# Column sums of modulation chunks: from TensorE products per accumulator to VectorE folds and shared products

## The chip, the cores and the metric

The kernel runs on one core of a Trainium2 chip. The metric is the device time of one execution in microseconds (us). Engines are named as in the profile: PE is TensorE, PEld its weight loads, DVE is VectorE, ACT is ScalarE, POOL is GpSimd, SP is the engine that issues most DMAs.

## The reference, cut to what matters

A decoder trunk of two layers on a sequence of 512 tokens with 1024 channels. Each layer is three sub-layers (feed-forward, token mixing, feed-forward), and each sub-layer is scaled, shifted and gated by values that come from a conditioning vector c. All of these modulation values of a layer are one vector-matrix product:

```python
c_act = jax.nn.silu(c)
for l in range(DEPTH):
    mod = (c_act @ w_ada[l] + b_ada[l]).reshape(bsz, 3, 3, D_MODEL)
    x = modulated_sublayer(x, ffn1, norm_g[l, 0], norm_g[l, 1], mod[:, 0], 0.5)
    x = modulated_sublayer(x, token_mixing, norm_g[l, 2], norm_g[l, 3], mod[:, 1], 1.0)
    x = modulated_sublayer(x, ffn2, norm_g[l, 4], norm_g[l, 5], mod[:, 2], 0.5)
```

Here w_ada[l] is 1024 by 9216, so a layer reads 36 MB of weights for 9216 numbers.

## The kernel before, in words

The 9216 columns of a layer are 18 chunks of 512. For a chunk, the 1024 rows of w_ada come as eight pieces of 128 rows by 512 columns. DVE multiplies each piece by its 128 values of silu(c), one per partition, and adds it to an accumulator AACC of 128 by 512 (`ada_pieces`, lines 1807 and 1810). What is left is the sum of the accumulator over its 128 partitions, with the result laid out as MOD: column 4 * chunk + q, partition p, holds element 128 q + p of the chunk. PE makes it (`ada`, line 933): four f32 products, each with 128 columns of AACC as the stationary operand and one column of ones as the moving one. DVE copies the four resulting columns from PSUM to MOD (`ada_columns`, line 1817).

The work is spread over the feed-forward stages, whose main work is matmuls of f32 split in a high and a low half, so that each product is three (`three`, lines 843 to 845). A feed-forward input stage (`ffn_in`) has 22 tiles, written (i, u) with i from 0 to 10 and u 0 or 1. A tile is 48 matmuls of 128 by 512. After the matmuls of a tile, ACT applies silu, DVE multiplies (line 1784, in `ffn_tile`), then makes the low half of the weights of two tiles later (line 1745; ACT makes the high half, line 1279), then the low half of the product (line 1788), and then takes four pieces of a modulation chunk. So each chunk takes two tiles of the stage. The order of every engine is written out by hand and held by semaphores. PE, after the second tile of step i, waits for the chunk of step i - 1 and makes its four products; DVE copies the columns one step later. SP loads weight groups and modulation pieces in one queue; the pieces go round through four buffers AW.

Stage by stage: layer 0's first five chunks are done ahead of and beside the first stage in another way (lines 612, 616, 925) that the change leaves alone. The first feed-forward stage of each layer does 11 chunks, ten of which have their products inside that stage, and the last in the token mixing (item 3, step 0 on PE; the copy at step 3 on DVE). The second feed-forward stage does 7 chunks in layer 0 (two of its own layer, five of the next) and 2 in layer 1. That is 31 chunks, 29 of them with their products in a feed-forward stage.

Two of the AW buffers and one accumulator lie over the part of the constants table CT that only the mixing stage uses. At the end of the first feed-forward stage SP waits until the chunks no longer need that space and loads the rest of CT (line 791), then goes on with weight groups. The first 256 columns of CT (identity and ones) are loaded at the very start (line 575). `columns` adds the bias to finished MOD columns and forms the gains PRE and POST of a sub-layer.

Of the kernel before, what the change touches and what calls it, by code (L numbers as in the profile page):

```python
# [8 lines left out]
F32 = mybir.dt.float32  # L9
# [6 lines left out]
P = 128  # L16
# [137 lines left out]
ADA_OWN = ADA_ALL - ADA_FIRST - ADA_CHUNKS[0]  # L154
ADA_BEFORE = (0, ADA_CHUNKS[0])


# [4 lines left out]

assert 4 * ADA_FIRST >= 2 * KT and 4 * (ADA_ALL - ADA_OWN) >= 8 * KT and ADA_OWN + ADA_FIRST == ADA_CHUNKS[1] and DEPTH == 2


CONST = {}
_at = 0
for _name, _n in (("ident", P), ("ones", P), ("ntri", P), ("nones", P), ("negm", P), ("strict", P),
                  ("reset", SEQ), ("del0", TT * 2 * P), ("del1", P), ("del2", P)):
    CONST[_name] = (_at, _n)  # L170
    _at += _n
# [12 lines left out]
def constants():  # L184
    t = np.zeros((P, NCONST), np.float32)
    i, j = np.arange(P)[:, None], np.arange(P)[None, :]

    def put(name, a):
        at, n = CONST[name]
        t[:, at:at + n] = np.broadcast_to(a, (P, n))  # L190

    put("ident", (i == j) * 1.0)
    put("ones", 1.0)
    put("ntri", (i >= j) * -1.0)
# [31 lines left out]
def body(nc, ctx, t, out):  # L226
# [31 lines left out]
    EPSC = sb("EPSC", [P, 1])  # L258
    NGR = sb("NGR", [P, A_V])
    phase = at[0]  # L260

# [12 lines left out]
    AACC = [sb("AACC0", [P, SEQ])]  # L274
    spare = CT_AT + 4 * 2 * P
    AW += [sb(f"AW{2 + i}", [P, SEQ], F32, spare + 2048 * i) for i in range(2)]
    AACC.append(sb("AACC2", [P, SEQ], F32, spare + 4096))

    AWB = [sb(f"AWB{i}", [P, KT, SEQ], F32, phase + 16384 * i) for i in range(FIRST_WAVE)]
# [92 lines left out]
    def at(sem, n):  # L372
# [22 lines left out]
    ada_part, ada_sum, ada_out, ada_cols = (  # L395
        sig("ada_part", 19 * KT), sig("ada_sum", 18), sig("ada_out", 18), sig("ada_cols", 10))

# [126 lines left out]

    def ada_bank(f, i):
        return 6 if (f, i) == (0, FI // 2 - 1) else 4 + i % 2

# [42 lines left out]
    with nc.Block() as block:  # L570
        @block.sync
        def _(sp):
            sp.dma_start(ROWS[0:8, :], t["c"].rearrange("o (k p) -> (o k) p", p=P)).then_inc(c_rows_in, 16)
            sp.dma_start(ROWS[8:20, :], t["hgrn_lb_logits"].rearrange("l (k p) -> (l k) p", p=P)).then_inc(c_rows_in, 16)
            sp.dma_start(CT[:, 0:2 * P], t["const_f"][:, 0:2 * P]).then_inc(const_in, 16)
            w = t["w_ada"].rearrange("l (k p) c -> p l k c", p=P)
# [147 lines left out]
    with nc.Block() as block:  # L724

            @block.sync
            def _(sp):
# [9 lines left out]
                def ffn(f, g0, name, g1, name_out):  # L737
# [102 lines left out]
            def _(pe):  # L840
# [57 lines left out]
                def ffn_in(p, f, g0):  # L898
                    def group(u):
                        wh = WH[(g0 + u) % 2][:, :].rearrange("p (k h c) -> p k h c", k=KT, h=2)  # L900
                        wl = WL[(g0 + u) % 2][:, :].rearrange("p (k h c) -> p k h c", k=KT, h=2)
                        for half in range(2):
                            for k in range(KT):
                                mm = three(PS[:, 2 * u + half, :], wh[:, k, half, :], wl[:, k, half, :],
                                           HH[:, k, :], HL[:, k, :], k == 0, k == KT - 1)
                            mm.then_inc((a_done, w_used)[half], 1)

                    first_pair(p, g0, lambda i: (a_done, w_used)[i])

# [74 lines left out]
                def ffn_out(f, g0, b):  # L984
# [4 lines left out]
                    def bank_free(j):  # L989
# [3 lines left out]
                        if j == 4:  # L993
                            pe.wait_ge(ada_out, at(ada_out, ADA_BEFORE[f] + chunks(l, f) - (chunks(l, f) == FI // 2)))
                        if j in (0, 2):
# [62 lines left out]
                def a_head(h, k):  # L1058
# [29 lines left out]
                    if k == 5:  # L1088
                        pe.wait_ge(i_kdt, at(i_kdt, h + 1))
                        pe.wait_ge(i_st, at(i_st, 3 * h))  # L1090
                        if h == 0:
                            pe.wait_ge(ada_out, at(ada_out, ADA_CHUNKS[0]))
                        for x in apart_before(TILE0[ITEM_HEAD[h + 1]], 6):
# [157 lines left out]
                for l in range(DEPTH):  # L1251
# [4 lines left out]
                    for m in range(2, NM):  # L1256
                        for k in range(8):
                            if (m, k) == (3, 0):
                                pe.wait_ge(*taken(6))
                                ada(0, ADA_CHUNKS[0] - 1)  # L1260
                            project(m, k)
# [10 lines left out]
            def _(act):  # L1272
# [255 lines left out]
                def mixers(m, k):  # L1528
# [13 lines left out]
                    if (m, k) == (ITEM_B + 1, 5):  # L1542
                        a_norm()
                        act.wait_ge(mix_const, at(mix_const, 16))
                        act.activation(CR[:, 0, :], ident, ACT.Copy)
                        act.activation(CR[:, 1:4, :], CT[:, 2 * P:5 * P].rearrange("p (n c) -> p n c", n=3), ACT.Copy).then_inc(c_round, 1)
                    hb = 2 * (m - (ITEM_B + 2)) + k // 4
# [63 lines left out]
            def _(dve):  # L1611
# [151 lines left out]
                def ffn_in(f, g0):  # L1763
                    n = chunks(l, f)
                    for i in range(FI // 2):
                        for u in range(2):
                            ffn_tile(f, g0, i, u)
                            if u == 0 and 1 < i <= n + 1:
                                ada_columns(f, i - 2)
                            if (i, u) == (FI // 2 - 1, 1) and n == FI // 2:  # L1770
                                ada_columns(f, i - 1)
                            if i < n:
                                ada_pieces(f, i, u)
                            if (l, f) == (0, 0) and 1 <= i <= 4:
                                extra_piece(2 * i + u - 2)
# [24 lines left out]
                def ada_pieces(f, i, u):  # L1800
                    for k in range(4 * u, 4 * u + 4):
# [3 lines left out]
                        if k == 0:  # L1805
                            dve.wait_ge(ada_sum, at(ada_sum, max(ADA_BEFORE[f] + i - 1, 0)))
                            ins = dve.tensor_scalar(acc, w, CC[:, k:k + 1], None, ALU.mult)
# [4 lines left out]

                def ada_columns(f, i):

                    dve.wait_ge(ada_sum, at(ada_sum, ADA_BEFORE[f] + i + 1))
                    ch = i + ADA_FIRST if f == 0 else i + ADA_ALL - ADA_OWN if i < ADA_OWN else i - ADA_OWN
                    dve.tensor_copy(MOD[:, 4 * ch:4 * ch + 4], PS[:, ada_bank(f, i), 0:4]).then_inc(ada_out, 1)

# [331 lines left out]
                for l in range(DEPTH):  # L2150
# [5 lines left out]
                    ffn_in(0, G_FFN1)  # L2156
                    dve.wait_ge(ada_out, at(ada_out, ADA_CHUNKS[0] - 1))
                    dve.wait_ge(first_out, ADA_FIRST)
                    columns(l, 4 * (ADA_FIRST if l else FIRST_WAVE), 4 * (ADA_ALL - ADA_OWN - 1), 2, (1,), (0, 1))
                    dve.wait_ge(ada_cols, at(ada_cols, 6))  # L2160
                    row_groups(G_FO1, FO - 2)
                    boundary(3 * l, G_MIX)
                    for m in range(2, NM):
                        for k in range(8):
                            if (m, k) == (3, 3):
                                ada_columns(0, ADA_CHUNKS[0] - 1)
                                dve.wait_ge(ada_out, at(ada_out, ADA_CHUNKS[0]))
                                columns(l, 4 * (ADA_ALL - ADA_OWN - 1), 4 * (ADA_ALL - ADA_OWN), 6, (2,), ())
                                dve.wait_ge(ada_cols, at(ada_cols, 8))
# [24 lines left out]
                    ffn_in(1, G_FFN2)  # L2194
                    dve.wait_ge(ada_out, at(ada_out, ADA_BEFORE[1] + chunks(l, 1)))
                    columns(l, 4 * (ADA_ALL - ADA_OWN), 72, 8, (), (2,))
# [60 lines left out]
```

## Time and profile before

| what | value |
|---|---|
| median of three runs | 2877.12 us (2877.07 to 2877.78) |
| span of the profiled execution | 2873.6 us |
| its own time | not listed apart; the lowest run is 3.5 us above the span |
| granted TensorE clock, mean | 0.994 |
| instructions | 36457 |

The span is the time from the first to the last instruction; the time of an execution also has some microseconds around it. In the rows below, a time in square brackets is how long the engine stood idle before the instruction, and what ended that. In a group of instructions the numbers after the bar are busy time in us, mean ns of one, and idle time before them. Matmul durations overlap: the distance between the starts of neighbours is what one costs in a full stream. An f32 product shows as two matmuls with two weight loads.

### The profile page before, as it was taken

The numbers are of one execution on the slowest core, as the hardware profiler recorded it, in microseconds if no ns is written. First come the engines' busy times: TensorE is split into PE (matmuls) and PEld (weight loads), VectorE is DVE, ScalarE is ACT, GpSimd is POOL, SyncE is SP. The second block draws the span as 40 slices with busy tenths as digits, with TensorE's granted clock in tenths as the row PEclk, the third lists the DMA queues.
The fourth block names the chain that finished last, engine by engine and source line by source line (L and its number), as shares of the span: only waits on it lengthen the run. The fifth ranks groups of instructions, "written<-read, shape, count | busy, mean of one in ns | idle before, by whom it ended". The sixth has DMA issues, their size and how long they took to land.

```text
span 2873.6 us, 36457 instructions
## 1 busy us (share of the span) xinstructions
PE 2813.7 (98%) x14737; PEld 2377.0 (83%) x14737; DVE 1570.7 (55%) x2389; ACT 1053.2 (37%) x1586; POOL 62.9 (2%) x54
## 2 busy tenths in 40 slices
PE   7999999999999999999999999999999999999998
PEld 6888888888888888888888888888888887888887
DVE  6655337787455456532275551588865545643323
ACT  4222145555422443222242221555553233522213
POOL 0000000000000110000000000000000002000000
PEclk9999999999999999999999999999999999999999
DMA  7655332222123244542336652322221232443321
GB/s 260 205 188 189 120 103 81 67 67 74 44 59 103 74 147 147 189 119 95 111 118 189 192 178 103 96 70 71 67 59 45 74 103 74 133 132 101 101 90 59
DMA packets 358857, 323.09 MB, mean 112 GB/s; under 512 B 12317, under 2 KB 305697, under 8 KB 357921
## 3 DMA queue, kind: packets, MB, share of 16 engines
q1 hardware_dynamic: 357152, 318.59, 34.9%
q8 instruction: 117, 1.92, 0.3%
q10 hardware_dynamic: 1536, 2.16, 0.3%
q14 instruction: 52, 0.42, 0.0%
HBM read 312.25 MB, written 6.29 MB: 111 GB/s over the span
## 4 chain that ended last, share of the span: by engine, by line
PE 88%; DVE 5%; ACT 3%; issue 2%; POOL 1%; DVEq 0%; POOLq 0%; ACTq 0%
PE PS L843 26%; PE PS L845 25%; PE PS L844 25%; PE PS L1074 2%; PE PS L1160 1%; PE PS L1137 1%; PE PS L1123 1%; PE PS L1182 1%; PE PS L933 1%; PE PS L1146 1%; PE PS L862 1%; ACT WH L1279 1%; PE PS L1168 1%; POOL MA L2233 1%; DVE MA L2186 1%
## 5 line engine op out<-in xcount | busy, mean ns | idle before, releaser
L843 PE MATMUL PS<-HH,WH 128*128 128x512 f32 (+1 forms) x2540 | 991.6, 390 | 25.7 <-DVE HL L1664 16.4
L845 PE MATMUL PS<-HH,WL 128*128 128x512 f32 (+1 forms) x2540 | 963.3, 379 | 0.0
L844 PE MATMUL PS<-HL,WH 128*128 128x512 f32 (+1 forms) x2540 | 962.1, 379 | 0.0
L843 PEld LDWEIGHTS PS<-HH,WH 128*128 128x128 f32 x2540 | 480.3, 189 | 121.2 <-DVE HL L1664 18.5
L1745 DVE TENSOR_TENSOR WL<-RAW,WH 128x2048 fp32r<-128x2048 f32 x142 | 325.4, 2292 | 436.9 <-ACT WH L1279 436.9
L845 PEld LDWEIGHTS PS<-HH,WL 128*128 128x128 f32 x2540 | 480.0, 189 | 91.1
L844 PEld LDWEIGHTS PS<-HL,WH 128*128 128x128 f32 x2540 | 480.7, 189 | 84.1 <-issue 2.9
L1279 ACT ACTIVATE WH<-RAW 128x2048 fp32r<-128x2048 f32 x142 | 271.7, 1914 | 691.3 <-PE PS L845 671.8
L843 PE MATMUL PS<-GH,WH 128*128 128x512 f32 (+1 forms) x696 | 262.4, 377 | 0.0
L845 PE MATMUL PS<-GH,WL 128*128 128x512 f32 (+1 forms) x696 | 262.4, 377 | 0.0
L844 PE MATMUL PS<-GL,WH 128*128 128x512 f32 (+1 forms) x696 | 261.7, 376 | 0.0
L1784 DVE TENSOR_TENSOR SB<-SB,PS 128x512 f32<-128x512 f32 x88 | 60.4, 687 | 328.9 <-PE PS L845 328.9
L1756 DVE TENSOR_TENSOR WL<-RAW,WH 128x512 fp32r<-128x512 f32 (+1 forms) x264 | 173.0, 680 | 121.1 <-ACT WH L1288 120.9
L1810 DVE SCALAR_TENSOR_TENSOR AACC<-AW,CC,AACC 128x512 f32<-128x512 f32 x217 | 162.9, 751 | 20.9 <-DMA AW<-in_w_ada 1.3
L1288 ACT ACTIVATE WH<-RAW 128x512 fp32r<-128x512 f32 (+1 forms) x264 | 146.3, 600 | 59.0 <-PE PS L845 30.9
L843 PEld LDWEIGHTS PS<-GH,WH 128*128 128x128 f32 x696 | 131.0, 188 | 26.0
L845 PEld LDWEIGHTS PS<-GH,WL 128*128 128x128 f32 x696 | 130.9, 188 | 26.1
L844 PEld LDWEIGHTS PS<-GL,WH 128*128 128x128 f32 x696 | 130.9, 188 | 26.1
L1400 ACT ACTIVATE SB<-PS 128x512 f32<-128x512 f32 x88 | 52.7, 599 | 267.2 <-PE PS L845 262.2
L1074 PEld LDWEIGHTS PS<-QL,KL 128*64 128x64 f32 (+5 forms) x576 | 62.6, 174 | 24.0 <-DVE QL L1955 12.7
L1515 ACT ACTIVATE CP<-CS 128x512 f32<-128x512 f32 x32 | 20.2, 633 | 160.9 <-DVE CS L2055 160.9
L843 PE MATMUL PS<-WH,HH 128*128 128x256 f32 x256 | 74.2, 290 | 0.0
(257 smaller groups left out, 3446.1 us busy)
## 6 DMA issues: line engine op xcount, KB each, us to landing
RAW<-in_ffn_w_in SPq DMA_DIRECT2D x176, 512.0 KB, 5.1
RAW<-in_w_in SPq DMA_DIRECT2D x132, 512.0 KB, 4.7
AW<-in_w_ada SPq DMA_DIRECT2D x248, 256.0 KB, 4.8
RAW<-in_ffn_w_out SPq DMA_DIRECT2D x88, 512.0 KB, 4.2
AWB<-in_w_ada SPq DMA_DIRECT2D x4, 2048.0 KB, 13.6
RAW<-in_w_out SPq DMA_DIRECT2D x16, 512.0 KB, 3.9
x_kept<-X SPq DMA_DIRECT2D x2, 2048.0 KB, 6.3
X<-x_kept SPq DMA_DIRECT2D x2, 2048.0 KB, 10.1
```

Source lines behind the costliest of these rows:

```text
L843: pe.matmul(o, ah, bh, start=start, stop=skip, skip_group_check=skip)
L844: pe.matmul(o, ah, bl, start=False, stop=skip, skip_group_check=skip)
L845: return pe.matmul(o, al, bh, start=False, stop=stop or skip, skip_group_check=skip)
L862: mm = pe.matmul(x_sum_at(half), ones, XSQ[q][:, 0, :], start=(q == 0), stop=True, skip_group_check=True)
L1074: mm = pe.matmul(PS[0:keys, 2 + n % 2, c * 64:(c + 1) * 64], KL[n % 2][:, c * P:c * P + keys], QL[n % 2][:, c, :], start=True, stop=True)
L1279: act.activation(halves_of(g)[0][:, 0:n], RAW[g % 2][:, 0:n], ACT.Copy).then_inc(w_high, 1)
L1288: act.activation(WH[slot][:, q * n:(q + 1) * n], RAW[slot][:, q * n:(q + 1) * n], ACT.Copy).then_inc(w_high if q == 3 else part_high, 1)
L1400: act.activation(SB[u][:, :], PS[:, 2 * u, :], ACT.Silu).then_inc(silu_done, 1)
L1745: dve.tensor_tensor(wl[:, 0:n], RAW[g % 2][:, 0:n], wh[:, 0:n].bitcast(F32), ALU.subtract).then_inc(w_low, PARTS)
L1756: dve.tensor_tensor(WL[slot][:, part], RAW[slot][:, part], WH[slot][:, part].bitcast(F32), ALU.subtract).then_inc(w_low, 1)
L1784: dve.tensor_tensor(SB[u][:, :], SB[u][:, :], PS[:, 2 * u + 1, :], ALU.mult).then_inc(gated, 1)
L1810: ins = dve.scalar_tensor_tensor(acc, w, CC[:, k:k + 1], acc, ALU.mult, ALU.add)
```

## The change

PE no longer sums each accumulator. When a chunk is complete, DVE transposes the accumulator in blocks of 32 by 32 into ATURN, and sums each run of 32 columns of that into one column (`ada_fold`): 16 columns, in which partition 32 r + j of column b holds the sum over the 32 partitions of quarter r of accumulator column 32 b + j. These 16 columns go to AFOLD (or ALATE for chunks 9 and 10 of a first feed-forward stage). One f32 product with a constant 128 by 128 matrix `fold` (1 where row and column agree modulo 32) as the stationary operand adds the four quarters of all chunks of a part at once. There are three parts in a layer: part 0 with nine chunks (144 columns) after tile (10, 0) of the first feed-forward stage, part 1 with two chunks (32 columns) at item 3, step 0 of the mixing, part 2 with the 7 or 2 chunks of the second feed-forward stage (112 or 32 columns) after tile (n + 1, 1), where n is their number. DVE copies a part into MOD with four copies of 32 partitions each (`ada_columns`; eight for the part whose chunks belong to two layers).

The fold of chunk i - 1 is placed after tile (i, 0) and ahead of that tile's pieces; the fold of the eleventh chunk comes at the end of the stage. An accumulator becomes free again when it is transposed. SP's load of the rest of CT waits for the last fold and for product 0. CT has 128 more columns, all in the part loaded at the start. Chunk 9's columns join MOD in the mixing and no longer in the feed-forward stage.

```diff
@@ PE @@
                             group(u)
-                            if u and i <= n:
-                                ada(f, i - 1)
+                            if (f, i, u) == (0, FI // 2 - 1, 0):
+                                ada(0)
+                            if (f, i, u) == (1, n + 1, 1):
+                                ada(2)
...
-                def ada(f, i):
-
-                    pe.wait_ge(ada_part, at(ada_part, i * KT + (ADA_BEFORE[f] + 2) * KT))
-                    pe.wait_ge(ada_out, at(ada_out, max(ADA_BEFORE[f] + i - 1, 0)))
-                    for q in range(4):
-                        mm = pe.matmul(PS[:, ada_bank(f, i), q:q + 1], AACC[i % 2][:, q * P:(q + 1) * P], ones[:, 0:1],
-                                       start=True, stop=True)
-                    mm.then_inc(ada_sum, 1)
+                def ada(part):
+
+                    bank, src, i0, count = ADA_AT[part]
+                    count = count or chunks(l, 1)
+                    pe.wait_ge(ada_folded, at(ada_folded, ADA_BEFORE[part // 2] + i0 + count))
+                    pe.matmul(PS[:, bank, 0:16 * count], const("fold"), src[:, 0:16 * count],
+                              start=True, stop=True).then_inc(ada_sum, 1)
@@ DVE @@
                             ffn_tile(f, g0, i, u)
-                            if u == 0 and 1 < i <= n + 1:
-                                ada_columns(f, i - 2)
-                            if (i, u) == (FI // 2 - 1, 1) and n == FI // 2:
-                                ada_columns(f, i - 1)
+                            if u == 0 and 1 <= i <= n:
+                                ada_fold(f, i - 1)
+                            if (f, i, u) == (0, FI // 2 - 1, 0):
+                                ada_columns(0)
+                            if (f, i, u) == (1, n + 2, 0):
+                                ada_columns(2)
                             if i < n:
                                 ada_pieces(f, i, u)
+                            if (i, u) == (n - 1, 1) and n == FI // 2:
+                                ada_fold(f, i)
...
+                def ada_fold(f, i):
+
+                    n = ADA_BEFORE[f] + i
+                    dst, c = folded_in(f, i)
+                    dve.wait_ge(ada_part, at(ada_part, (n + 2) * KT))
+                    dve.wait_ge(ada_folded, at(ada_folded, n))
+                    dve.transpose(ATURN[:, :], AACC[i % 2][:, :]).then_inc(ada_turned, 1)
+                    dve.wait_ge(ada_turned, at(ada_turned, n + 1))
+                    dve.tensor_reduce(dst[:, 16 * c:16 * c + 16], ATURN[:, :].rearrange("p (b j) -> p b j", j=32),
+                                      AX.X, ALU.add).then_inc(ada_folded, 1)
+
+                def ada_columns(part):
+
+                    bank, _, i0, count = ADA_AT[part]
...
+                        for r in range(4):
+                            rows = slice(32 * r, 32 * r + 32)
+                            ins = dve.tensor_copy(MOD[rows, 4 * ch:4 * (ch + n)],
+                                                  PS[rows, bank, 16 * c:16 * (c + n)].rearrange("p (c r) -> p r c", r=4)[:, r, :])
+                    ins.then_inc(ada_out, 1)
@@ SP @@
-            sp.dma_start(CT[:, 0:2 * P], t["const_f"][:, 0:2 * P]).then_inc(const_in, 16)
+            sp.dma_start(CT[:, 0:3 * P], t["const_f"][:, 0:3 * P]).then_inc(const_in, 16)
...
-                        sp.wait_ge(ada_part, at(ada_part, KT * (ADA_CHUNKS[0] + 1)))
-                        sp.wait_ge(ada_out, at(ada_out, ADA_CHUNKS[0] - 1))
-                        c = 2 * P
+                        sp.wait_ge(ada_folded, at(ada_folded, ADA_CHUNKS[0]))
+                        sp.wait_ge(ada_sum, at(ada_sum, 1))
+                        c = 3 * P
                         sp.dma_start(CT[:, c:], t["const_f"][:, c:]).then_inc(mix_const, 16)
```

## Rows read from the trace of the kernel before

**Rows 1.** The page's first part: busy time and share of the span by engine.

```profile
PE 2813.7 (98%) x14737; PEld 2377.0 (83%) x14737; DVE 1570.7 (55%) x2389; ACT 1053.2 (37%) x1586; POOL 62.9 (2%) x54
```

**Rows 2.** Waits of PE over the whole span: total us, times, longest.

```profile
PE PS L843 <- DVE HL L1664: 16.4, 11, 2.6
PE PS L1074 <- DVE QL L1955: 6.3, 7, 1.9
```

**Rows 3.** Groups by line: the removed products, the pieces, the removed copies.

```profile
L933 PE MATMUL PS<-CT,AACC 128*128 128x1 f32 x248 | 29.4, 240 | 0.0
...
L1810 DVE SCALAR_TENSOR_TENSOR AACC<-AW,CC,AACC 128x512 f32<-128x512 f32 x217 | 162.9, 751 | 20.9 <-DMA AW<-in_w_ada 1.3 <-DVE AACC L1810 0.5
...
L1817 DVE COPY MOD<-PS 128x4 f32<-128x4 f32 x31 | 4.8, 153 | 0.0
```

**Rows 4.** Timeline of PE around one chunk's products: start us, us, instruction.

```profile
113.97 0.39 PE L845 MATMUL PS<-HH,WL 128*128 128x512 f32 x1
114.19 0.95 PE L933 MATMUL PS<-CT,AACC 128*128 128x1 f32 x8
115.00 0.49 PE L843 MATMUL PS<-HH,WH 128*128 128x512 f32 x1
115.33 0.40 PE L844 MATMUL PS<-HL,WH 128*128 128x512 f32 x1
```

**Rows 5.** Timeline of DVE over two tiles of layer 0's first feed-forward stage.

```profile
240.79 0.69 DVE L1784 TENSOR_TENSOR SB<-SB,PS 128x512 f32<-128x512 f32 x1 [3.69 <-PE PS L845]
242.80 2.29 DVE L1745 TENSOR_TENSOR WL<-RAW,WH 128x2048 fp32r<-128x2048 f32 x1 [1.32 <-ACT WH L1279]
...
245.61 0.15 DVE L1817 COPY MOD<-PS 128x4 f32<-128x4 f32 x1
...
246.26 2.46 DVE L1810 SCALAR_TENSOR_TENSOR AACC<-AW,CC,AACC 128x512 f32<-128x512 f32 x3
251.67 0.69 DVE L1784 TENSOR_TENSOR SB<-SB,PS 128x512 f32<-128x512 f32 x1 [2.94 <-PE PS L845]
...
263.50 0.69 DVE L1784 TENSOR_TENSOR SB<-SB,PS 128x512 f32<-128x512 f32 x1 [3.70 <-PE PS L845]
```

**Rows 6.** Timeline of DVE, layer 1's second feed-forward stage, two tiles without products.

```profile
2580.37 0.69 DVE L1784 TENSOR_TENSOR SB<-SB,PS 128x512 f32<-128x512 f32 x1 [5.90 <-PE PS L845]
...
2591.25 0.69 DVE L1784 TENSOR_TENSOR SB<-SB,PS 128x512 f32<-128x512 f32 x1 [5.98 <-PE PS L845]
```

**Rows 7.** Timeline of PE in the mixing: two f32 passes of 512 columns.

```profile
468.37 0.39 PE L845 MATMUL PS<-HH,WL 128*128 128x512 f32 x1
468.60 1.02 PE L1064 MATMUL PS<-QB,CT 128*128 128x512 f32 x2
...
469.69 0.40 PE L844 MATMUL PS<-HL,WH 128*128 128x512 f32 x1
```

**Rows 8.** Groups by line, DVE: a sum along 512 columns, a one-source operation.

```profile
L2053 DVE TENSOR_REDUCE OC<-CS 128x2 f32<-128x512 f32 (+1 forms) x32 | 22.0, 688 | 1.1
...
L1900 DVE TENSOR_SCALAR W<-W 128x512 f32<-128x512 f32 x12 | 5.0, 416 | 0.0
```

**Rows 9.** Timeline of PE, mixing of layer 0, after item 3's products.

```profile
471.68 0.68 PE L1074 MATMUL PS<-QL,KL 128*64 128x64 f32 x8 [0.67 <-DVE QL L1955]
...
479.46 1.02 PE L1074 MATMUL PS<-QL,KL 128*120 128x64 f32 x8
```

**Rows 10.** Timeline of DVE, same stretch.

```profile
476.42 0.15 DVE L1817 COPY MOD<-PS 128x4 f32<-128x4 f32 x1
...
477.94 0.42 DVE L1955 TENSOR_TENSOR QL<-AQ,AE 128x256 f32<-128x256 f32 x1
```

**Rows 11.** DMA issues: the constants at the start, KB, us to landing.

```profile
CT<-in_const_f SPq DMA_DIRECT2D x1, 128.0 KB, 2.1
```

**Rows 12.** Busy times, clock, DMA share and GB/s in a stretch of the start.

```profile
20.00:35.00 15.00, 13.52 (x66) 11.15 (x67) 10.23 (x22) 9.08 (x17) 0.00 (x0) 0.90 1.09 376
```

**Rows 13.** Timeline of DVE at the end of layer 0's first feed-forward input stage.

```profile
311.18 2.29 DVE L1745 TENSOR_TENSOR WL<-RAW,WH 128x2048 fp32r<-128x2048 f32 x1 [5.42 <-ACT WH L1279]
```

More of the change, by code:

```diff
@@ L155 @@
 ADA_BEFORE = (0, ADA_CHUNKS[0])
+ADA_LATE = 2
+ADA_EARLY = ADA_CHUNKS[0] - ADA_LATE
 def chunks(l, f):
     return ADA_OWN if f and l == DEPTH - 1 else ADA_CHUNKS[f]
-assert 4 * ADA_FIRST >= 2 * KT and 4 * (ADA_ALL - ADA_OWN) >= 8 * KT and ADA_OWN + ADA_FIRST == ADA_CHUNKS[1] and DEPTH == 2
+assert 4 * ADA_FIRST >= 2 * KT and 4 * (ADA_ALL - ADA_OWN - ADA_LATE) >= 6 * KT and 4 * (ADA_ALL - ADA_OWN) >= 8 * KT and ADA_OWN + ADA_FIRST == ADA_CHUNKS[1] and DEPTH == 2
 CONST = {}
 _at = 0
-for _name, _n in (("ident", P), ("ones", P), ("ntri", P), ("nones", P), ("negm", P), ("strict", P),
+for _name, _n in (("ident", P), ("ones", P), ("fold", P), ("ntri", P), ("nones", P), ("negm", P), ("strict", P),
                   ("reset", SEQ), ("del0", TT * 2 * P), ("del1", P), ("del2", P)):
@@ L193, in constants @@
     put("ones", 1.0)
+    put("fold", (i % 32 == j % 32) * 1.0)
     put("ntri", (i >= j) * -1.0)
@@ L259, in body @@
     NGR = sb("NGR", [P, A_V])
+    ALATE = sb("ALATE", [P, ADA_LATE * 16])
     phase = at[0]
@@ L274, in body @@
     AACC = [sb("AACC0", [P, SEQ])]
-    spare = CT_AT + 4 * 2 * P
+    spare = CT_AT + 4 * 3 * P
     AW += [sb(f"AW{2 + i}", [P, SEQ], F32, spare + 2048 * i) for i in range(2)]
     AACC.append(sb("AACC2", [P, SEQ], F32, spare + 4096))
+    ATURN = sb("ATURN", [P, SEQ], F32, spare + 6144)
+    AFOLD = sb("AFOLD", [P, ADA_EARLY * 16], F32, spare + 8192)
+    assert spare + 8192 + 64 * ADA_EARLY <= CT_AT + 4 * NCONST
     AWB = [sb(f"AWB{i}", [P, KT, SEQ], F32, phase + 16384 * i) for i in range(FIRST_WAVE)]
@@ L395, in body @@
     ada_part, ada_sum, ada_out, ada_cols = (
-        sig("ada_part", 19 * KT), sig("ada_sum", 18), sig("ada_out", 18), sig("ada_cols", 10))
+        sig("ada_part", 19 * KT), sig("ada_sum", 3), sig("ada_out", 3), sig("ada_cols", 10))
+    ada_turned, ada_folded = sig("ada_turned", 18), sig("ada_folded", 18)
     y_done, y_copied, y_sq, y_pair = (sig(n) for n in ("y_done", "y_copied", "y_sq", "y_pair"))
@@ L523, in turns_until, with folded_in @@
         return sum(x < tile for x in TURN_OF)
-    def ada_bank(f, i):
-        return 6 if (f, i) == (0, FI // 2 - 1) else 4 + i % 2
+    ADA_AT = ((5, AFOLD, 0, ADA_EARLY), (6, ALATE, ADA_EARLY, ADA_LATE), (5, AFOLD, 0, None))
+    def folded_in(f, i):
+        late = f == 0 and i >= ADA_EARLY
+        return (ALATE, i - ADA_EARLY) if late else (AFOLD, i)
     def cols_of(half, e):
@@ L993, in bank_free @@
                         if j == 4:
-                            pe.wait_ge(ada_out, at(ada_out, ADA_BEFORE[f] + chunks(l, f) - (chunks(l, f) == FI // 2)))
+                            pe.wait_ge(ada_out, at(ada_out, 3 if f else 1))
                         if j in (0, 2):
@@ L1091, in a_head @@
                         if h == 0:
-                            pe.wait_ge(ada_out, at(ada_out, ADA_CHUNKS[0]))
+                            pe.wait_ge(ada_out, at(ada_out, 2))
                         for x in apart_before(TILE0[ITEM_HEAD[h + 1]], 6):
@@ L1259, in _ @@
                                 pe.wait_ge(*taken(6))
-                                ada(0, ADA_CHUNKS[0] - 1)
+                                ada(1)
                             project(m, k)
@@ L1545, in mixers @@
                         act.activation(CR[:, 0, :], ident, ACT.Copy)
-                        act.activation(CR[:, 1:4, :], CT[:, 2 * P:5 * P].rearrange("p (n c) -> p n c", n=3), ACT.Copy).then_inc(c_round, 1)
+                        act.activation(CR[:, 1:4, :], CT[:, 3 * P:6 * P].rearrange("p (n c) -> p n c", n=3), ACT.Copy).then_inc(c_round, 1)
                     hb = 2 * (m - (ITEM_B + 2)) + k // 4
@@ L1805, in ada_pieces @@
                         if k == 0:
-                            dve.wait_ge(ada_sum, at(ada_sum, max(ADA_BEFORE[f] + i - 1, 0)))
+                            dve.wait_ge(ada_turned, at(ada_turned, max(ADA_BEFORE[f] + i - 1, 0)))
                             ins = dve.tensor_scalar(acc, w, CC[:, k:k + 1], None, ALU.mult)
@@ L1811, in ada_pieces @@
                         ins.then_inc(ada_part, 1)
[L1813 to L1817, printed above, removed]
+                def ada_fold(f, i):
[9 more added lines that the diff above has]
+                    bank, _, i0, count = ADA_AT[part]
+                    count = count or chunks(l, 1)
+                    dve.wait_ge(ada_sum, at(ada_sum, part + 1))
+                    if part < 2:
+                        runs = [(ADA_FIRST + i0, 0, count)]
+                    else:
+                        runs = [(ADA_ALL - ADA_OWN, 0, ADA_OWN)]
+                        if count > ADA_OWN:
+                            runs.append((0, ADA_OWN, count - ADA_OWN))
+                    for ch, c, n in runs:
+                        for r in range(4):
[3 more added lines that the diff above has]
+                    ins.then_inc(ada_out, 1)
                 def take(m, i):
@@ L2156, in _ @@
                     ffn_in(0, G_FFN1)
-                    dve.wait_ge(ada_out, at(ada_out, ADA_CHUNKS[0] - 1))
+                    dve.wait_ge(ada_out, at(ada_out, 1))
                     dve.wait_ge(first_out, ADA_FIRST)
-                    columns(l, 4 * (ADA_FIRST if l else FIRST_WAVE), 4 * (ADA_ALL - ADA_OWN - 1), 2, (1,), (0, 1))
+                    columns(l, 4 * (ADA_FIRST if l else FIRST_WAVE), 4 * (ADA_ALL - ADA_OWN - ADA_LATE), 2, (1,), (0, 1))
                     dve.wait_ge(ada_cols, at(ada_cols, 6))
@@ L2165, in _ @@
                             if (m, k) == (3, 3):
-                                ada_columns(0, ADA_CHUNKS[0] - 1)
-                                dve.wait_ge(ada_out, at(ada_out, ADA_CHUNKS[0]))
-                                columns(l, 4 * (ADA_ALL - ADA_OWN - 1), 4 * (ADA_ALL - ADA_OWN), 6, (2,), ())
+                                ada_columns(1)
+                                dve.wait_ge(ada_out, at(ada_out, 2))
+                                columns(l, 4 * (ADA_ALL - ADA_OWN - ADA_LATE), 4 * (ADA_ALL - ADA_OWN), 6, (2,), ())
                                 dve.wait_ge(ada_cols, at(ada_cols, 8))
@@ L2194, in _ @@
                     ffn_in(1, G_FFN2)
-                    dve.wait_ge(ada_out, at(ada_out, ADA_BEFORE[1] + chunks(l, 1)))
+                    dve.wait_ge(ada_out, at(ada_out, 3))
                     columns(l, 4 * (ADA_ALL - ADA_OWN), 72, 8, (), (2,))
```

## The prediction, made before the changed kernel was run

> **What bounds the kernel now.** I read first the page's busy times: PE is busy for 98% of the span, DVE for 55%, ACT for 37% [rows 1]. Then the waits of PE: the largest add up to 16.4 us (for HL, at the boundaries between sub-layers) and 6.3 us (for QL, in the mixing) [rows 2]; in the feed-forward stages, where this change does nearly all its work, PE does not wait tile by tile. So PE's stream sets the end there, and what is taken out of it comes off the time, unless a later engine becomes the new limit. Then the groups by line: the products that go are 248 matmuls, eight for each of 31 chunks [rows 3]. Their busy time, 29.4 us, is not their price, since matmul durations overlap. The price is read from the timeline of DVE, where each tile begins with the multiply that waits for PE's last matmul: a tile without products takes 251.67 - 240.79 = 10.88 us, a tile with them 263.50 - 251.67 = 11.83 us [rows 5], and two tiles of the stage's quiet end are 10.88 us apart as well [rows 6]. So a chunk's products cost 0.95 us. PE's own timeline agrees: from the matmul before the products to the second one behind them it is 115.33 - 113.97 = 1.36 us [rows 4], against two steps of 10.88 / 48 = 0.227 us, which leaves 0.91 us.
>
> **Removed from PE in the feed-forward stages.** 29 chunks have their products there: 29 x 0.95 = 27.5 us, all on the path.
>
> A chunk is eight passes of one moving column, so a pass costs 0.95 / 8 = 0.119 us; two passes of 512 columns cost 0.87 us [rows 7], as worked out below, or 0.00085 us a column. A pass of one column costs 140 times that, so the rows do not price these products by their moving columns. The Trainium skill ("TensorE: Matmul & The Clock Gate", Back-to-back issue gap) does price an isolated matmul by them, with some 25 ns for 64 or fewer. As an estimate from that page, the 29 chunks would cost 29 x 8 x 0.025 = 5.8 us, and the change would gain about that and no more; rows 5 contradict this. Pricing by columns stays as a rival below.
>
> **Added to PE.** Four products of two f32 passes in the feed-forward stages: 144, 112, 144 and 32 columns. From below, two of the eight passes above: 0.24 us. From above, two passes of 512 columns: 469.69 - 468.37 = 1.32 us less two steps of 0.227, 0.87 us [rows 7]. I go by columns between 1 and 512: 0.42, 0.38, 0.42 and 0.28 us, together 1.5 us (ends 1.0 and 3.5). None waits for its inputs: product 0 needs chunk 8, folded a whole step of two tiles earlier, and part 2's product stands three tiles behind its last fold.
>
> **Added to DVE, a fold a chunk.** The transpose is in no row of this trace. Nearest is a 1x operation of the same shape, the sum along 512 columns: 0.69 us [rows 8]; as the low end the fast one-source operation, 0.42 us [rows 8]; as the high end 64 blocks of 32 by 32, each at the 0.153 us of the smallest copy [rows 3], 9.8 us. I take 0.69, as it reads and writes 512 columns as that row reads them. The reduce is that row's own operation: 0.69. A fold is 1.4 us. Its cover: behind the pieces DVE stands idle 2.94 us before the next multiply [rows 5], and the removed copy gives back some 0.07 us more, so 3.0 us. The fold delays the pieces, the release of AW buffers and SP's next loads by 1.4 us. A piece fetched then is used a tile (10.88 us) later, and the four buffers are refilled one by one, so nothing late reaches PE. If the cover were gone, the multiply would be late, but PE next needs the low weights that DVE makes two tiles ahead: they end 242.80 + 2.29 - 240.79 = 4.30 us into a tile of 10.88, so another 6.6 us pass before PE stands still. Cost: nothing.
>
> **The stage's last fold** comes behind the last pieces, 1.4 us; behind it on DVE stand `columns` and the low weights of the out projection. DVE then waited 5.42 us for the high half of those [rows 13]. The four small copies of part 0 (0.153 us each at most) lie in tile (10, 0)'s cover. SP's wait for the last fold holds back the rest of CT and the weight groups 4 and later of the out projection by the same 1.4 us; those groups wait for low weights that come after the fold on DVE anyway, and CT is first read in the mixing. Nothing.
>
> **The mixing, twice.** Eight passes become two of 32 columns: PE gets 0.95 - 0.28 = 0.67 us less. But behind it PE waits 0.67 us for DVE's QL [rows 9], and DVE is busy without a break there, so PE only comes earlier to the same wait: nothing gained (upper end 0.67 each). DVE's copies rise from one to four, at most 3 x 0.153 = 0.46 us more; the QL after them was ready at 477.94 + 0.42 = 478.36, used by PE at 479.46 [rows 9, 10], 1.1 us of cover. Nothing lost (lower end 0.46 each).
>
> **The start.** The first load of constants grows from 128 to 192 KB [rows 11]. The queues move 376 GB/s there, with the DMA engines' share above 1 [rows 12]: 65.5 KB are 0.17 us, and the first matmuls wait for weights behind them in the queue. I take 0.2 us; ends 0 and 1.05 us (half of that load's 2.1 us).
>
> **Sum.** -27.5 + 1.5 + 0.2 = -25.8 us: the span of 2873.6 us goes to 2847.8. The execution's own time is not listed apart; the three runs lie within 0.7 us, and their median is 3.5 us above the span, which I keep: 2851.3 us, 0.9% less.
>
> **Rivals.**
> *The mixing gives some back.* There DVE is the limit for stretches, as the wait in rows 9 shows. If the longer copies hold up QL every time, twice 0.46 us, and the four products cost their high end, 3.5 us, it is 2.9 us more: 2854.2 us, and with the start's high end 2855.1. For it: DVE without idle time in rows 10's stretch. Against: 1.1 us of cover.
> *The removed passes are cheap.* If passes were paid by their moving columns (0.00085 us each), and the extra 0.95 us of every second tile belonged to the pair of tiles, 29 x 8 columns would give 0.2 us and the four products' 2 x 432 columns cost 0.7 us: 2877.1 - 0.2 + 0.7 + 0.2 = 2877.8 us. Against: rows 6, where two tiles without products show no extra time. This is the mechanism of the page's issue gap.
> *Slower: the fold makes DVE the limit.* Place: every step of two tiles that carries a chunk. DVE's work of a tile is 251.67 - 2.94 - 240.79 = 7.94 us, of which 1.32 us is a wait for ACT that vanishes once DVE is late [rows 5], so 2 x 6.6 = 13.2 us a pair against PE's new 21.8. It decides from a fold of 8.5 us on. At the transpose's high end the fold is 10.5 us, the pair 23.7 instead of 22.7, so 29 x 1.0 = 29 us more: 2906 us. Against: no row of that shape is above 0.75 us [rows 3, 8].
> That the change does not do what it says would leave 248 one-column matmuls in place; the diff shows one product a part, so I give that nothing.
>
> **How the numbers follow.** Forecast 0.86, mixing and products at their high ends 0.08, cheap passes 0.03, slow fold 0.03. A measurement tells 0.2%, 5.8 us, from no change. The forecast and the first rival are faster: 0.94; the cheap passes, at 0.7 us slower, lie within the bound: 0.03; slow fold: 0.03. The range's low end: products 1.0, both mixings gained (1.34), no cost at the start: -27.8, 2849.3 us, less the runs' 0.7: 2848.5. High end: 2855.1 plus 0.7, rounded up: 2856.0. Left out are the last two rivals, 0.06, and what I did not see.
>
> **What would show it.** Right: line 933's group gone and 12 longer matmuls in its place; multiplies of a chunk's second tile 10.88 us after the first and again to the next; transposes and reduces near 0.69 us, with some 1.6 us of DVE idle time left before the multiply; in the mixing the wait for QL grown by about 0.6 us. Wrong: waits of PE for WL in the feed-forward stages, tiles still at 11.8 us, or a transpose of several us.

## The result, and the profile after

The changed kernel takes 2842.5 us (median; before 2877.1 us in the same comparison), a ratio of 0.988 with a 95% interval of 0.9865 to 0.9895. One more run of it took 3946.3 us, and one of `a_phase512` below 4632.8 us, at a mean granted clock of 0.654 and 0.556; these two slow runs are left out of every time here. The forecast of a gain was right; its size was not: 34.6 us less where 25.8 us were forecast, outside the range of 2848.5 to 2856.0 us. The profiled run took 2843.08 us with a span of 2841.3 us.

The page's first part, the waits of PE, and the groups by line of the new instructions, all of the changed kernel (the code has moved by some lines: 855 to 857 are the three matmuls, 947 the new product, 1836 and 1838 the fold):

```profile
PE 2776.7 (98%) x14501; PEld 2353.0 (83%) x14501; DVE 1614.7 (57%) x2448; ACT 1053.2 (37%) x1586; POOL 62.8 (2%) x54
```

```profile
PE PS L855 <- DVE HL L1677: 15.6, 6, 2.6
PE PS L1087 <- DVE QL L1995: 7.6, 7, 1.9
...
PE PS L1087 <- DVE AS L1971: 1.5, 2, 0.8
```

```profile
L947 PE MATMUL PS<-AFOLD,CT 128*128 128x144 f32 (+2 forms) x8 | 1.5, 266 | 0.0
...
L947 PE MATMUL PS<-ALATE,CT 128*128 128x32 f32 x4 | 0.6, 234 | 0.0
...
L1836 DVE STREAM_TRANSPOSE ATURN<-AACC 128x512 f32<-128x512 f32 x31 | 21.9, 705 | 0.1
...
L1838 DVE TENSOR_REDUCE AFOLD<-ATURN 128x16 f32<-128x512 f32 x27 | 18.5, 686 | 0.9
```

The one-column group of [rows 3] is gone, 12 matmuls stand in its place, and a fold is 0.705 + 0.686 us. The wait for AS is new against [rows 2]. The timeline of DVE over two tiles, which answers to [rows 5], and the tile with product 0:

```profile
236.53 0.69 DVE L1801 TENSOR_TENSOR SB<-SB,PS 128x512 f32<-128x512 f32 x1 [2.75 <-PE PS L857]
...
241.35 0.70 DVE L1836 STREAM_TRANSPOSE ATURN<-AACC 128x512 f32<-128x512 f32 x1
242.09 0.69 DVE L1838 TENSOR_REDUCE AFOLD<-ATURN 128x16 f32<-128x512 f32 x1
...
247.41 0.69 DVE L1801 TENSOR_TENSOR SB<-SB,PS 128x512 f32<-128x512 f32 x1 [1.68 <-PE PS L857]
...
258.29 0.69 DVE L1801 TENSOR_TENSOR SB<-SB,PS 128x512 f32<-128x512 f32 x1 [2.75 <-PE PS L857]
...
280.05 0.69 DVE L1801 TENSOR_TENSOR SB<-SB,PS 128x512 f32<-128x512 f32 x1 [2.75 <-PE PS L857]
...
291.22 0.69 DVE L1801 TENSOR_TENSOR SB<-SB,PS 128x512 f32<-128x512 f32 x1 [1.13 <-PE PS L857]
```

Every tile now takes 10.88 us, the idle time left behind the fold is 1.68 us, and the tile behind product 0 takes 291.22 - 280.05 = 11.17 us, so the 144-column product costs 0.29 us. All of this is much as forecast. So the other 8.8 us must come from a stage that the forecast did not look at. Lengths of stages, from the first to the last matmul of each in the timelines of PE, us:

| stretch of PE's work | before | after | difference |
|---|---|---|---|
| feed-forward input, layer 0, first | 227.00 | 218.76 | -8.24 |
| its out projection, 512 columns | 103.02 | 100.42 | -2.60 |
| feed-forward input, layer 0, second | 224.05 | 217.68 | -6.37 |
| its out projection, 512 columns | 103.34 | 100.42 | -2.92 |
| feed-forward input, layer 1, first | 225.95 | 217.69 | -8.26 |
| its out projection, 512 columns | 103.02 | 100.41 | -2.61 |
| feed-forward input, layer 1, second | 219.30 | 217.68 | -1.62 |
| its out projection, 512 columns | 103.35 | 100.42 | -2.93 |

The four out projections give 11.1 us, and not one instruction of them was changed. The stretch view counts their matmuls in 80 us of layer 0's second out projection, first before, then after (PE and its count, PEld, DVE, ACT, POOL, clock, DMA share, GB/s):

```profile
1330.00:1410.00 80.00, 80.00 (x345) 64.36 (x344) 16.05 (x7) 13.41 (x7) 0.00 (x0) 1.00 0.28 100
```

```profile
1317.00:1397.00 80.00, 80.00 (x355) 66.24 (x354) 16.20 (x8) 13.41 (x7) 0.00 (x0) 1.00 0.31 105
```

At the same full clock, with the same work on the other engines, 355 matmuls fit where 345 did. In the timelines of PE, neighbours there start 0.2267 us apart in place of 0.2333.

What differs is the place of the operands in SBUF, the memory in which the kernel lays out its tensors. CT grew by 512 bytes and ALATE takes 128, so the area behind them, which begins with GH, moved by 640 bytes: GH from byte 127488 to 128128. GH, GL and YH are moving operands there, the side of a product with 512 columns. The weights WH and WL, the stationary side with 128 columns, did not move (WH at 82048). Two theories: **the place** of the moving operand sets the distance of matmuls; or **a state** of PE's stream, in which the one-column products leave a slower pace behind them.

### The profile page after: what moved, and what is told of

It is laid out like the page before. It is cut to its first block, busy times and chain, and to the rows that moved or that the text cites. A ratio compares the mean times of both kernels' runs of the same rounds, so it can differ in the third digit from the quotient of the medians.

```text
span 2841.3 us, 36046 instructions
## 1 busy us (share of the span) xinstructions
PE 2776.7 (98%) x14501; PEld 2353.0 (83%) x14501; DVE 1614.7 (57%) x2448; ACT 1053.2 (37%) x1586; POOL 62.8 (2%) x54
## 4 chain that ended last, share of the span: by engine, by line
PE 88%; DVE 5%; ACT 3%; issue 2%; POOL 1%; DVEq 0%; POOLq 0%; ACTq 0%
PE PS L855 26%; PE PS L857 25%; PE PS L856 25%; PE PS L1087 2%; PE PS L1173 1%; PE PS L1150 1%; PE PS L1136 1%; PE PS L1195 1%; PE PS L1159 1%; PE PS L874 1%; ACT WH L1292 1%; PE PS L1181 1%; POOL MA L2273 1%; DVE MA L2226 1%; DVE HL L1677 0%
## 5 line engine op out<-in xcount | busy, mean ns | idle before, releaser
L1087 PE MATMUL PS<-QL,KL 128*64 128x64 f32 (+5 forms) x576 | 65.8, 257 | 9.2 <-DVE QL L1995 7.6
```

The source lines that it names most:

```text
L1087: mm = pe.matmul(PS[0:keys, 2 + n % 2, c * 64:(c + 1) * 64], KL[n % 2][:, c * P:c * P + keys], QL[n % 2][:, c, :], start=True, stop=True)
```

## The experiments

**Before, with the area moved.** `b_pad640`, on the kernel before:

```diff
+    at[0] += 640
     phase = at[0]
```

> The kernel before, with 640 bytes left free ahead of the area that begins with GH, so that GH, GL, YH and the rest of that area lie where the change puts them; no instruction differs. Layout theory (the place of GH and YH sets the distance of their matmuls): that distance falls from 0.232-0.233 to 0.2267 us, each of four out projections is 2.6 to 2.9 us shorter, in all 11 to 12.5 us less: 2864.5 to 2866 us. State theory (the one-column products leave PE's stream in a slower pace, and the change removes them): distance unchanged, 2877 us. The tiles with products stay at 11.83 us under both.

Measured: 2865.2 us against 2877.5, ratio 0.9961 (0.9947 to 0.9976): 12.3 us less without any change of instructions. The same 80 us of the out projection:

```profile
1331.00:1411.00 80.00, 80.00 (x355) 66.24 (x354) 16.16 (x8) 13.41 (x7) 0.00 (x0) 1.00 0.30 105
```

The place theory holds, and the state theory falls: all one-column products are still there.

**After, with the area moved back.** `a_phase512`, on the changed kernel:

```diff
-    MOD = sb("MOD", [P, 72])
...
     AACC = [sb("AACC0", [P, SEQ])]
+    at[0] = phase + 100992
+    MOD = sb("MOD", [P, 72])
...
```

> The changed kernel, with 640 bytes of small tensors (MOD, PRE, POST, LBW, OML, EPSC) moved behind everything else, so that the area of GH begins at the byte where it began before the change; no instruction differs. Layout theory: distance back at 0.233 us in the out projections, 11 to 12.5 us more than the changed kernel's 2842.6: 2853.5 to 2855 us, so the fold by itself is worth 22 to 23.5 us. State theory: 2842.6 us, distance 0.2267.

Measured: 2850.5 us, ratio to the kernel before 0.9905 (0.9888 to 0.9922). The same count:

```profile
1317.00:1397.00 80.00, 80.00 (x345) 64.34 (x344) 16.21 (x8) 13.41 (x7) 0.00 (x0) 1.00 0.29 98
```

Each out projection is back at 103.35 us, 2.93 us more. This kernel is what the prediction was about, the fold with the operands of the out projections in their old places, and it stands 0.8 us from the forecast of 2851.3. It came out 3 us and more under what was expected of it from the changed kernel's time, a point taken up below.

**Everything moved together.** `a_all128`, on the changed kernel:

```diff
-    base = (nc.sbuf_base + 31) // 32 * 32
+    base = (nc.sbuf_base + 31) // 32 * 32 + 128
```

> The changed kernel with every tensor 128 bytes further on (HH, WH and GH from 128 to 256 modulo 1024). If the distance of matmuls depends on the moving operand's place relative to the stationary one: unchanged, 2842.6 us. If it depends on the moving operand's place by itself: HH's and GH's matmuls both go to 0.233 us or to some third distance; at 0.233 that is 0.0066 x some 9400 matmuls of 512 columns, 60 us more.

Measured in a single run: 2838.7 us, some 4 us under the unchanged time expected, and the fast count. Its first feed-forward stage began at 41.38 us, that of the changed kernel's profile at 44.04 us, a point taken up below as well.

```profile
1312.00:1392.00 80.00, 80.00 (x355) 66.24 (x354) 16.22 (x8) 13.41 (x7) 0.00 (x0) 1.00 0.31 105
```

So it is not the moving operand's place by itself.

**The matmul by itself.** `micro_place`, a stream of the kernel's own matmuls:

```python
for s in STATION:
    for m in MOVING:
        for i in range(24):
            w = s // 4 + P * (i % 8)
            mm = pe.matmul(PS[:, n % 8, :], WT[:, w:w + P], MV[:, m // 4:m // 4 + 512], start=True, stop=True)
            n += 1
```

> Nothing of the reference is computed: the output is a copy of x. A stream of matmuls of the kernel's own shape (128x128 weights, 512 columns, fp32r), 24 for each of 32 places of the moving operand (0 to 1984 bytes in steps of 64) times four places of the stationary one (0, 128, 64, 512 bytes), both counted from a multiple of 2048. Layout theory: the distance differs between places, 0.227 us at some and 0.233 at others, and the table says whether the moving place or the difference of the two counts. State theory: one distance for all places.

Measured, as the mean distance in ns between the starts of the matmuls of a group of 24, from its third to its last, for the first 256 bytes of the moving place; the numbers repeat every 256 bytes up to 1984, but for the very first group (226.7):

```text
moving place   stationary at 0   at 128   at 64   at 512
0 (256, ...)        227.2        232.4    233.3    227.2
64                  229.0        233.3    227.2    229.0
128                 232.4        227.2    229.0    232.4
192                 233.3        229.0    232.4    233.3
```

Down each diagonal the number is the same: what counts is moving place less stationary place, modulo 256. At 0 it is 227.2, at 64 229.0, at 128 232.4, at 192 233.3 ns. Before the change GH less WH was 45440 = 177 x 256 + 128; after it, 46080 = 180 x 256. HH less WH is a multiple of 256 in both, and the input stages ran at the fast distance all along: a tile of 48 matmuls read 10.88 us. Why the distance depends on this difference, no run shows.

**In finer steps.** `micro_fine`: the same stream with the stationary operand at 0 and `MOVING = tuple(range(0, 256, 4))`.

> Nothing of the reference is computed: the output is a copy of x. The same stream with the stationary operand at 0 and the moving one at 0 to 252 bytes in steps of 4, 24 matmuls each. From the coarse table (227.2, 229.0, 232.4 and 233.3 ns at differences of 0, 64, 128 and 192 modulo 256): if these are steps of 64 bytes, four levels; if the cost follows the difference smoothly, a ramp, and some difference just below 256 may be cheaper than 227.

Measured: neither four levels nor a ramp. The 64 places scatter between 226.7 and 240.0 ns; 226.7 occurs at 0, 28, 60, 156, 236 and 240, and 240.0 at 20, 196 and 244. No place is faster than 226.7 ns, so the changed kernel's places, at 0.2267 us, have nothing left to give. The order of the fine values stays unexplained.

**The rule put to the test.** `b_pad128` and `b_pad64`: the kernel before with 128 or 64 in place of 640.

> The kernel before with 128 bytes left free ahead of GH's area: GH at 127616, a multiple of 256 behind the stationary weights (WH at 82048). If the difference of the two places modulo 256 is what counts (as in the stream of matmuls by themselves), 128 bytes do what 640 did: 0.2267 us a matmul in the out projections, 2865 us. If 640 bytes helped in another way (a bank or a row at a larger step), 2877 us.

> The same with 64 bytes: a difference of 192 modulo 256, the dearest of the four coarse places (233.3 ns against 232.4 at the kernel's 128). If the difference counts: 0.2333 us a matmul, 2877 to 2879 us. If any move helps: 2865 us.

Measured: 2865.5 us for 128 bytes (ratio 0.9958, 0.9942 to 0.9975) and 2877.3 us for 64 bytes (a single run). The counts, 128 bytes first:

```profile
1331.00:1411.00 80.00, 80.00 (x355) 66.26 (x354) 16.04 (x7) 13.41 (x7) 0.00 (x0) 1.00 0.30 105
```

```profile
1331.00:1411.00 80.00, 80.00 (x344) 64.13 (x343) 16.92 (x12) 13.41 (x7) 0.00 (x0) 1.00 0.28 94
```

128 bytes do all that 640 did, 64 bytes do nothing.

**How much fold the stage can hide.** `a_turn8` and `a_turn14`, on the changed kernel, with 8 or 14 more transposes in each fold:

```diff
+                    for r in range(8):
+                        dve.transpose(ATURN[:, :], AACC[i % 2][:, :]).then_inc(ada_turned, 1)
+                        dve.wait_ge(ada_turned, at(ada_turned, 9 * n + r + 1))
                     dve.transpose(ATURN[:, :], AACC[i % 2][:, :]).then_inc(ada_turned, 1)
```

> The changed kernel with eight more transposes of the same accumulator ahead of each fold's own, a fold of some 7.3 us in place of 1.4 us on VectorE. By the bound worked out in the prediction (the fold decides from 8.5 us on, since the multiply is late from 3.0 us on, but TensorE waits for the low weights only 6.6 us later): unchanged, 2843 us within 3 us, tiles still 10.88 us. Rival (the cover is only the idle time ahead of the multiply, 3.0 us): 29 x 4.3 = 125 us more, 2968 us.

> The same with fourteen more transposes, a fold of some 11.8 us. By the bound: VectorE's pair of tiles takes 13.2 + 11.8 = 25.0 us against TensorE's 21.8, so 29 x 3.2 = 93 us more, some 2936 us, and TensorE waits for WL. Rival of the small cover: 29 x 8.8 = 255 us more, 3098 us.

Measured in a single run each: 2844.8 us with 8, 2943.0 us with 14. The timeline of DVE with 8:

```profile
237.06 0.69 DVE L1801 TENSOR_TENSOR SB<-SB,PS 128x512 f32<-128x512 f32 x1
...
241.88 5.93 DVE L1837 STREAM_TRANSPOSE ATURN<-AACC 128x512 f32<-128x512 f32 x8
...
252.16 0.68 DVE L1801 TENSOR_TENSOR SB<-SB,PS 128x512 f32<-128x512 f32 x1
...
258.82 0.69 DVE L1801 TENSOR_TENSOR SB<-SB,PS 128x512 f32<-128x512 f32 x1
```

DVE has no idle time ahead of its multiplies any more, and the one at 252.16 is 15.1 us behind the one at 237.06; yet the pair still takes 258.82 - 237.06 = 21.76 us, PE's own pace. With 14, the waits of PE and the timeline of DVE over one pair:

```profile
PE PS L855 <- DVE WL L1758: 52.3, 29, 4.0
...
PE PS L855 <- DVE SB L1801: 13.9, 2, 6.9
PE PS L939 <- DVE AACC L1814: 8.5, 1, 8.5
```

```profile
240.42 0.68 DVE L1801 TENSOR_TENSOR SB<-SB,PS 128x512 f32<-128x512 f32 x1
243.82 10.41 DVE L1837 STREAM_TRANSPOSE ATURN<-AACC 128x512 f32<-128x512 f32 x14
...
255.01 0.69 DVE L1841 TENSOR_REDUCE AFOLD<-ATURN 128x16 f32<-128x512 f32 x1
...
265.21 0.68 DVE L1801 TENSOR_TENSOR SB<-SB,PS 128x512 f32<-128x512 f32 x1
```

The pair takes 265.21 - 240.42 = 24.79 us (25.0 expected), and PE waits for WL. The time is 7 us above the 2936 us expected; PE also waits 13.9 us for SB and 8.5 us for an accumulator there, which the expectation did not have. The fold in this run takes 255.70 - 243.82 = 11.88 us, so DVE's other work of a pair is 12.91 us, and the fold decides from 21.76 - 12.91 = 8.85 us on, where 8.5 us were worked out. The slow-fold rival had its mechanism right and its threshold nearly so; the real fold of 1.4 us is just far from it.

**The mixing's new wait.** In the changed kernel the timelines of PE and of DVE, which answer to [rows 9, 10]:

```profile
463.98 0.68 PE L1087 MATMUL PS<-QL,KL 128*64 128x64 f32 x8 [1.29 <-DVE QL L1995]
...
472.42 1.02 PE L1087 MATMUL PS<-QL,KL 128*120 128x64 f32 x8 [0.75 <-DVE AS L1971]
```

```profile
468.73 0.68 DVE L1855 COPY MOD<-PS 32x8 f32<-32x8 f32 x4
469.44 0.17 DVE L1628 TENSOR_TENSOR MOD<-MOD,COLS 128x8 f32<-128x8 f32 x1
...
471.84 0.43 DVE L1971 COPY_PREDICATED AS<-LM,PS 96x256 f32<-96x256 uint8 x1
```

The wait for QL grew from 0.67 to 1.29 us, the 0.6 us that PE came earlier. Then PE waits 0.75 us more: line 1971 empties the PSUM bank that the next product needs, and it is late. `a_late` takes two short instructions, the bias and the gains of the mixing, from in front of it:

```diff
                                 ada_columns(1)
                                 dve.wait_ge(ada_out, at(ada_out, 2))
-                                columns(l, 4 * (ADA_ALL - ADA_OWN - ADA_LATE), 4 * (ADA_ALL - ADA_OWN), 6, (2,), ())
-                                dve.wait_ge(ada_cols, at(ada_cols, 8))
...
+                    columns(l, 4 * (ADA_ALL - ADA_OWN - ADA_LATE), 4 * (ADA_ALL - ADA_OWN), 6, (2,), ())
+                    dve.wait_ge(ada_cols, at(ada_cols, 8))
                     row_groups(G_WO, 2)
```

> The changed kernel with the bias and gains of the mixing part (one add and one product of some 0.17 us each, 0.4 us with their waits) moved from item 3, step 3 of the mixing to just ahead of the output projection's weight lows, where VectorE waits for ScalarE. If the new 0.75 us wait of TensorE for AS comes from VectorE being later by the three added copies (0.71 us in place of 0.18): that wait falls by about 0.4 us in each layer, 0.8 us less in all, below what a comparison of times can tell; the trace shows it. If the wait has another cause, it stays at 0.75 us.

Measured: 2841.0 us (ratio to the kernel before 0.9871, 0.9855 to 0.9888), and the wait:

```profile
469.80 1.02 PE L1087 MATMUL PS<-QL,KL 128*120 128x64 f32 x8 [0.34 <-DVE AS L1971]
```

0.75 became 0.34 us, the fall of some 0.4 us that was expected. The time is 1.5 us under the changed kernel's, which is within the scatter of the runs.

## Why the prediction was wrong in size

*The removed products* (27.5 us less) and *the added ones* (1.5 us): right. The table's input stages give 8.24 + 6.37 + 8.26 + 1.62 = 24.5 us, and two chunks whose products stood between an input stage and its out projection 0.82 and 0.81 us; together 26.1 us, against 27.5 - 1.5 = 26.0. The product of 144 columns cost 0.29 us, nearer to its low end of 0.24 than to the 0.42 taken. Pricing the one-column passes by their moving columns is refuted by the tiles' fall from 11.83 to 10.88 us.

*The fold* was costed at nothing, with 0.69 us a transpose; it measured 0.705 us, and the cover was as worked out, which the two kernels with longer folds show at both sides of the threshold.

*The mixing* was costed at nothing on the ground that QL had 1.1 us of cover. That looked at the wrong successor: PE's matmul there also waits for the copy that empties its bank. The timeline of DVE of the kernel before has it in the stretch of [rows 10]; a row from its feed-forward stage [rows 5] stands ahead, for the copies below:

```profile
245.68 0.47 DVE L1807 TENSOR_SCALAR AACC<-AW,CC 128x512 f32<-128x512 f32 x1
...
476.60 0.16 DVE L1615 TENSOR_TENSOR MOD<-MOD,COLS 128x4 f32<-128x4 f32 x1
...
478.88 0.43 DVE L1931 COPY_PREDICATED AS<-LM,PS 96x256 f32<-96x256 uint8 x1
```

That copy ended at 479.31, and PE started at 479.46 [rows 9], 0.15 us later. In the changed kernel, where PE waits for it, the distance is 0.15 us as well (472.42 - 471.84 - 0.43), so there was no cover at all. From the first matmul behind item 3's products to this start PE took 1.28 us more in layer 0 and 1.26 us more in layer 1, while the products took 0.66 us less: 0.6 us lost a layer, where the sum had nothing. The four copies took 469.44 - 468.73 = 0.71 us to the next instruction, where the single one took 476.60 - 476.42 = 0.18 us. The Trainium skill ("VectorE: DVE Perf Modes", Two Vector instructions with no wait between them) has an instruction held back until the earlier ones have finished when its input or its output starts in another quarter of the partitions than the last one's. The trace agrees: the four copies start in four quarters and follow each other at 0.16 to 0.18 us, each behind the end of the one before, while the single copy at 245.61 [rows 5], 0.15 us long, let the next instruction start after 0.07 us, at 245.68.

*The start*: the step that failed. It said that CT grows by 128 columns and priced the 64 KB of the load at 0.2 us. That term came to nothing: PE's first product starts 0.3 us later (4.02 us against 3.72), but `a_phase512`, with the same 192 KB, began its first feed-forward stage at 41.60 us, the kernel before at 41.65 us. What it did not ask is what lies behind CT. The same 512 bytes, with ALATE's 128, moved every tensor of the feed-forward and mixing area, and with it the moving operand of 1776 matmuls in the out projections and 384 in the branch products (0.5 us shorter a layer). The place by itself is worth 12.3 us, as the kernel before with 640 bytes of nothing shows. The fold by itself is worth 27.0 us (2850.5 against 2877.5), inside the range. That this is so near to 25.8 us is in part luck: the mixing lost 1.2 us that the sum did not have, and the spans of the two profiled runs differ by 2873.6 - 2848.8 = 24.8 us.

The two parts add up to 39.3 us, against the measured 34.6. Where the other 4.7 us went can be followed in the profiles of the changed kernel and of `a_phase512`, which hold the same instructions and come from executions within 0.6 us of the medians. Taken stretch by stretch, the moved operands make the changed kernel 12.0 us shorter there (11.5 us in the out projections with the short matmuls behind them, 0.5 us in the branch products), yet the spans differ by only 2848.8 - 2841.3 = 7.5 us.

2.4 us of the difference were lost at the start: the first feed-forward stage began at 44.04 us in the changed kernel's profile and at 41.60 us in that of `a_phase512`. 1.4 us of them were there by 32.72 us, behind a wait of PE of 0.88 us for an accumulator, where `a_phase512` had no wait (31.34 us). The granted clock fell to half at 32.6 us in both, so the eight matmuls that follow took 1.73 us to the next group in place of 0.91. From 20 to 30 us, before the change, in the changed kernel and in `a_phase512`, the DMA moved (last number, GB/s):

```profile
20.00:30.00 10.00, 8.66 (x42) 7.42 (x43) 5.41 (x12) 8.15 (x15) 0.00 (x0) 1.00 1.05 408
```

```profile
20.00:30.00 10.00, 7.77 (x36) 6.68 (x36) 4.46 (x11) 7.49 (x14) 0.00 (x0) 1.00 1.05 379
```

```profile
20.00:30.00 10.00, 8.48 (x39) 7.24 (x40) 5.51 (x13) 7.99 (x15) 0.00 (x0) 1.00 1.05 409
```

The fold is not the reason for the lower rate, as `a_phase512` has it too, and `b_pad640`, without it, has 379 GB/s and begins its first stage at 42.95 us.

The other 2.2 us went to the clock. Behind PE's waits of some 2.6 us at the boundaries between sub-layers, and once behind a wait of 1.9 us inside the mixing, the granted clock falls from 2.4 to 1.2 GHz for a short while, at some of these places in a run and not at others. The stretch at the end of layer 0, before and after the change:

```profile
1453.00:1482.00 29.00, 26.12 (x205) 24.98 (x204) 22.36 (x47) 16.95 (x31) 0.00 (x0) 1.00 0.06 17
```

```profile
1437.00:1467.00 30.00, 27.16 (x200) 26.01 (x199) 22.83 (x48) 16.60 (x30) 0.00 (x0) 0.94 0.08 23
```

The stretch with a mean of 0.94 took 29.79 us from first to last matmul, the one with 1.00 28.24 us: 1.55 us for one such fall. Between the changed kernel and `a_phase512` the falls differ at four places:

| stretch in the changed kernel, us | its mean clock | clock of `a_phase512` in the same stretch | changed kernel longer by, us |
|---|---|---|---|
| 616 to 620, mixing of layer 0 | 0.57 | 1.00 | 0.66 |
| 1454 to 1468, boundary | 0.88 | 1.00 | 1.54 |
| 1828 to 1832, boundary | 0.57 | 1.00 | 1.27 |
| 2474 to 2486, boundary | 1.00 | 0.88 | -1.24 |

So 12.0 - 2.4 - 2.2 = 7.4 us are left, against 7.5. `a_all128`, with the changed kernel's differences of places and an early start, came out 38.7 us under the kernel before of its comparison (2838.7 against 2877.5), close to the sum of the parts. What sets the DMA's rate at the start, and at which boundaries the clock falls, no run shows.

Last, the 3.5 us kept between span and time was too much: the runs with a span on record have some 1.8 us around it, the changed kernel's profiled run among them, so by that the run profiled before lay 1.7 us below the median of its kernel.

## What to carry to other kernels

When a change adds a constant or a buffer, list what lies behind it in memory and treat each moved operand as a part of the change; to measure an idea apart from its layout, run it once with the old addresses, and run the old kernel with the new ones. A stream of matmuls that loads its weights each time is worth one check of moving place less stationary place modulo 256: with multiples of 64 bytes, a multiple of 256 was the fastest here, for nothing but padding. Cover is the time to the first instruction that waits, so look for every successor of the delayed work, the one that frees a bank among them.

## What the runs showed of the hardware

The distance of fp32r matmuls of 512 columns, each with its own load of 128 weight columns, depends on the two operands' places in SBUF: 227.2, 229.0, 232.4 and 233.3 ns at differences of 0, 64, 128 and 192 bytes modulo 256, at all four stationary and 32 moving places tried; in steps of 4 bytes, with the stationary operand at one place, it scatters up to 240.0 and does not fall below 226.7 ns. A VectorE transpose of 128x512 f32 in 32x32 blocks takes 705 ns, like a sum over the same elements (686 ns). An f32 product of 144 columns cost 0.29 us of TensorE's time between two full streams, while eight one-column passes with their weight loads cost 0.95 us. Four VectorE copies into four quarters of the partitions follow each other at 0.16 to 0.18 us.
